# Attention softmax: mask, minimum and sign in one VectorE instruction, masks made by GpSimd

## The chip, the cores and the metric

The kernel runs on one core of one Trainium2 chip. The metric is the device time of one launch in microseconds (us), given as the median of several runs. A profiled execution is one launch recorded by the hardware profiler; its *span* reaches from its first to its last instruction, and its own time is a little longer. Five engines work side by side: TensorE (PE; its weight loads are PEld), VectorE (DVE), ScalarE (ACT), GpSimd (POOL, called Pool below) and SyncE (SP), which here only issues DMAs.

## What is computed

Two small models run in one launch, in float32, on 256 tokens of width 1024, batch 1. The first has two layers of feed-forward networks, a mixer with neighbourhood attention and an mLSTM, and a gating mixer. The second has a mixer of two attentions, a mixture of 16 experts, a mixer of two other attentions, and a second mixture. What matters here is the softmax of the five attentions, each with 8 heads of 64:

```python
# neighbourhood attention (NA): own keys in a window with a bias, and 256 context keys without one
s_loc = einsum('bqhd,baqkhd->bhqak', q_i, k_win) * scale + bias
s_ctx = einsum('bqhd,bchd->bhqc', q_i, kx) * scale
p = softmax(concatenate([s_loc, s_ctx]))
# sliding window with sinks (sw)
logits = logits - slopes * dist;  logits = where(valid, logits, -inf)
p = softmax(concatenate([logits, sink]))[..., :-1]
# causal with forget gates (fo); without them for the latent attention (la)
logits = logits + c_i[..., :, None] - cum[:, :, None, :]
p = softmax(where(pos[None, :] <= t[:, None], logits, -inf))
# selected keys (ds): the 64 best of each query by an index score
logits = logits - slopes * dist;  logits = where(dist >= 0, logits, -inf)
p = softmax(logits)
```

The slopes of `sw` and `ds` are 2 to the power -(h + 1) for head h.

## The kernel before

Each engine has a program written out by hand (`tensor_program`, `scalar_program`, `vector_program`, `pool_program`, `sync_program`), and the order in it is the order of the text. Engines wait for each other by counted semaphores: `w.wait_ge(result, ...)` waits for TensorE, `dve_out` for VectorE, `act_out` for ScalarE, `pool_out` for Pool, `const_in` and `bias_in` for DMAs. `then_inc(...)` announces an instruction's end. `behind()` on VectorE waits for all of its own earlier instructions.

The weights stream through the kernel. SyncE loads a piece into one of four `raw` buffers (512 or 2048 elements in each of 128 partitions), ScalarE copies it to `wh`, rounded to a shorter float type (L1410), VectorE takes the difference as `wl` (L2076), and TensorE multiplies with both: activations are split into `hh` and `hl` likewise, so each product is three matrix multiplications (L412). A `raw` buffer is free when `wl` is made.

An attention is a row of *units*: one head times one block of 128 queries. `NA` has 16 units with 512 keys (256 own, 256 context). `EV` has 32, 16 of `sw` and then 16 of `fo`; `OD` has 32, 16 of `la` and then 16 of `ds`. In these, the first block of queries has 128 keys and the second 256. The generator `attention(...)` stands in three programs, and `attend(n)` runs it on by n units between the pieces of the projections that go on at the same time; in `OD`, `pump(n)` puts instructions of the top-64 selection (eight largest, L2851, and their replacement, L2855) between them. For unit u:

- TensorE writes the logits into `banks[u % 2]` when the exponential of unit u-2 is done.
- VectorE adds the mask in place, in the bank: NA at L2419 with a bias that a separate instruction has summed (L2412, bias and window mask, a unit ahead), `sw` at L2766, `fo` at L2770, `la` at L2956, `ds` at L2960. Then it takes the maximum over the bank (`tensor_reduce`, L2343) and changes its sign (L2349; with sinks L2347, which takes the larger of maximum and sink too). The results lie in `st`, rows 0 and 1.
- ScalarE computes exp(bank + st row 1) into `E`, and its accumulator's sum into row 2 (L1553, which shows as two instructions).
- In step u+2 TensorE turns `E` (L649) and ScalarE copies it to `ET` (L1545); in step u+4 TensorE multiplies with the values.
- After 8 units VectorE makes reciprocals (L2360, with sinks L2356 and L2358 around an exponential of ScalarE) and scales the bank into `Y` (L2364). TensorE turns `Y` (L674), and `hl` of it is made by VectorE (L2795, L2974) for the output projection. In NA, VectorE copies the keys `kT` from a bank for each group of units (L2405); in EV ScalarE makes `e_va` and `e_vb` (L1797, L1805).

Pool loads constants (`load`, L3207), clears buffers (`zero`, L3216), keeps a ring of modulation weights filled, issues the 16 bias DMAs of NA (L3245, one in each unit, when the sum of the unit two before is done), and copies `o_kr` to `o_kz` (L3277). `phase(...)` makes it wait for the end of a phase before it loads into the room that the phase used.

Of the kernel before, what the change touches and what calls it, by code (L numbers as in the profile page):

```python
# [55 lines left out]
class Counting:  # L56
# [7 lines left out]
    tensor_tensor_scan = reciprocal = match_replace = max = nothing  # L64
# [55 lines left out]
def program(nc, dram):  # L120
# [5 lines left out]
    def sb(where, name, shape, dt=F32):  # L126
        return where.enter_context(nc.sbuf_tensor(name, shape, dt))
# [79 lines left out]
    with ExitStack() as mx:  # L207
# [4 lines left out]
        with ExitStack() as ph:  # L212
# [3 lines left out]
            na.bias = sb(ph, "bias", [P, 2, 2, T])  # L216
# [54 lines left out]
    with ExitStack() as mx:  # L271
# [16 lines left out]
        ev.on8 = sb(mx, "e_on8", [8, T])  # L288
        ev.cc = sb(mx, "e_cc", [P, 2, 8])
# [1106 lines left out]
    def scalar_program(e):  # L1396
# [139 lines left out]
        def attention(name, units, a):  # L1536
            for u in range(len(units) + 4):
# [8 lines left out]
                if u < len(units):  # L1546
# [6 lines left out]
                    e.activation(a.E[:, u % 4, 0:n], banks[u % 2][:, 0:n], ACT.Exp, bias=a.st[:, 1, c:c + 1],  # L1553
# [509 lines left out]
    def vector_program(e):  # L2063
# [34 lines left out]
        def behind():  # L2098
            w.wait_ge(dve_out)
# [232 lines left out]
        def attention(name, units, a, logits, out):  # L2332
            for u in range(len(units) + 4):
                if u < len(units):
# [4 lines left out]
                    mx, nm = a.st[:, 0, c:c + 1], a.st[:, 1, c:c + 1]  # L2339
                    w.wait_ge(result, "logit", name, u)  # L2340
                    logits(u, kd, qb, h, b)
                    behind()
                    e.tensor_reduce(mx, b[:, 0:n], AX.X, ALU.max).then_inc(*dve_out("mx", name, u))  # L2343
                    behind()
                    if kd == "sw":
                        w.wait_ge(const_in["sinks"], 0)
# [46 lines left out]
        def mixer0():  # L2393
# [21 lines left out]
            def logits(u, kd, qb, h, b):  # L2415
                if u == 0:
                    bias_sum(0)
                w.wait_ge(dve_out, "bias sum", u)
                e.tensor_tensor(b[:, 0:T], b[:, 0:T], na.bias[:, 1, u % 2, :], ALU.add).then_inc(*dve_out("biased", u))  # L2419
                if u < 15:  # L2420
                    bias_sum(u + 1)
# [6 lines left out]
            st.units = attention("na", NA, na.a, logits, out)  # L2428
# [298 lines left out]
        def even_mixer():  # L2727
# [33 lines left out]
            def logits(u, kd, qb, h, b):  # L2761
                n = P * (qb + 1)
                if kd == "sw":
                    slope = -float(np.float32(2.0) ** np.float32(-(h + 1)))
                    w.wait_ge(const_in["swdist"], 0)
                    e.scalar_tensor_tensor(b[:, 0:n], ev.swm[:, qb, 0:n], slope, b[:, 0:n], ALU.mult, ALU.add).then_inc(*dve_out("ev biased", u))  # L2766
                else:
                    w.wait_ge(const_in["causal"], 0)
                    w.wait_ge(dve_out, "ecc")
                    e.scalar_tensor_tensor(b[:, 0:n], b[:, 0:n], ev.cc[:, qb, h:h + 1], ev.cam[:, qb, 0:n], ALU.add,  # L2770
                                           ALU.add).then_inc(*dve_out("ev biased", u))
# [15 lines left out]
            st.units = attention("ev", EV, ev.a, logits, out)  # L2787
# [100 lines left out]
        def odd_mixer():  # L2888
# [63 lines left out]
            def logits(u, kd, qb, h, b):  # L2952
                n = P * (qb + 1)
                if kd == "la":
                    w.wait_ge(const_in["causal2"], 0)
                    e.tensor_tensor(b[:, 0:n], b[:, 0:n], od.cam[:, qb, 0:n], ALU.add).then_inc(*dve_out("od biased", u))  # L2956
                    return
                slope = -float(np.float32(2.0) ** np.float32(-(h + 1)))
                w.wait_ge(dve_out, "dd")
                e.scalar_tensor_tensor(b[:, 0:n], od.dd[:, qb, 0:n], slope, b[:, 0:n], ALU.mult, ALU.add).then_inc(*dve_out("od biased", u))  # L2960

            st.units = attention("od", OD, od.a, logits, lambda g: heads_of(od.Y, g % 2, 512 if g < 2 else 0))
# [239 lines left out]
    def pool_program(e):  # L3202
# [18 lines left out]

        def mod(n):
# [41 lines left out]
        pool_out.mark("ev zero")  # L3264
        for l, before in ((0, "even phase"), (1, "odd phase")):
# [247 lines left out]
```

## Time and profile before

| | us |
|---|---|
| median of 3 runs | 2475.62 (2473.22 to 2476.98) |
| profiled execution, its own time | 2474.83 |
| its span | 2472.9 |
| TensorE busy | 2328.4 (94% of the span) |
| VectorE busy | 1740.1 (70%) |
| ScalarE busy | 1197.9 (48%) |
| Pool busy | 115.7 (5%) |
| mean granted TensorE clock | 0.973 of full speed |

All times inside the execution count from the start of the span. Pool's share is that of its whole work, DMA issues among it. A `busy` of TensorE counts matrix products that wait for nothing, at whatever clock; the granted clock is 1.00 at 2.4 GHz and 0.5 at 1.2 GHz. The NA units lie between 526 and 587 us, the EV units between 1506 and 1606, the OD units between 2031 and 2090, so all the attentions together are some 220 us of the span.

In an entry such as `[1.32 <-DVE kT L2405]` the first number is the idle time in front of the instruction, and behind the arrow stands what released it.

### The profile page before, as it was taken

The numbers are of one execution on the slowest core, as the hardware profiler recorded it, in microseconds if no ns is written. First come the engines' busy times: TensorE is split into PE (matmuls) and PEld (weight loads), VectorE is DVE, ScalarE is ACT, GpSimd is POOL, SyncE is SP. The second block draws the span as 40 slices with busy tenths as digits, with TensorE's granted clock in tenths as the row PEclk, the third lists the DMA queues.
The fourth block names the chain that finished last, engine by engine and source line by source line (L and its number), as shares of the span: only waits on it lengthen the run. The fifth ranks groups of instructions, "written<-read, shape, count | busy, mean of one in ns | idle before, by whom it ended". The sixth has DMA issues, their size and how long they took to land.

```text
span 2472.9 us, 33815 instructions
## 1 busy us (share of the span) xinstructions
PE 2328.4 (94%) x14128; PEld 2038.2 (82%) x14128; DVE 1740.1 (70%) x2355; ACT 1197.9 (48%) x1549; POOL 115.7 (5%) x205
## 2 busy tenths in 40 slices
PE   7999999899989999999999998979999888899997
PEld 3778888778779999998999997868888687688886
DVE  4997777754776666666666655668888777688886
ACT  3222222334544454455554443457666555576665
POOL 0111111010000000000000010000000100000000
PEclk9999999999999999999999998989999989999999
DMA  7777887433115454455445552239988621389884
GB/s 273 230 243 254 269 265 262 130 132 110 69 58 182 171 205 169 172 205 216 153 160 177 180 199 102 99 108 330 349 311 316 259 103 52 124 341 345 317 311 167
DMA packets 80533, 501.71 MB, mean 203 GB/s; under 512 B 9584, under 2 KB 10688, under 8 KB 28656
## 3 DMA queue, kind: packets, MB, share of 16 engines
q1 hardware_dynamic: 59120, 423.66, 46.7%
q0 software_dynamic: 21248, 75.75, 9.7%
q8 instruction: 115, 1.88, 0.3%
q14 instruction: 50, 0.41, 0.1%
HBM read 498.33 MB, written 1.05 MB: 202 GB/s over the span
## 4 chain that ended last, share of the span: by engine, by line
PE 61%; DVE 22%; ACT 11%; issue 4%; DMA 2%; DVEq 0%; SPq 0%; ACTq 0%
PE bank L412 60%; DVE wl L2076 9%; ACT wh L1410 7%; DVE macc L2112 1%; ACT s L1511 1%; DVE f L2293 1%; DMA mring<-in_wmod 1%; DVE s L2284 1%; DMA raw<-in_wmod 1%; PE bank L1282 1%; DMA raw<-in_wstream 1%; DVE rs L2136 1%; PE bank L649 0%; DVE hl L2268 0%; DVE st_od L2343 0%
## 5 line engine op out<-in xcount | busy, mean ns | idle before, releaser
L2076 DVE TENSOR_TENSOR wl<-raw,wh 128x2048 fp32r<-128x2048 f32 (+1 forms) x437 | 905.0, 2077 | 378.1 <-ACT wh L1410 374.1
L1410 ACT ACTIVATE wh<-raw 128x2048 fp32r<-128x2048 f32 (+1 forms) x437 | 756.3, 1738 | 301.3 <-PE bank L412 295.1
L412 PE MATMUL bank<-hh,wh 128*128 128x258 f32 (+2 forms) x2200 | 691.7, 314 | 34.2 <-ACT o_rl L1839 5.3
L412 PE MATMUL bank<-hh,wl 128*128 128x258 f32 (+2 forms) x2200 | 675.2, 307 | 0.0
L412 PE MATMUL bank<-hl,wh 128*128 128x258 f32 (+2 forms) x2200 | 673.9, 306 | 0.0
L412 PEld LDWEIGHTS bank<-hh,wh 128*128 128x128 f32 x2200 | 422.1, 192 | 63.8 <-DVE hl L2714 6.0
L412 PEld LDWEIGHTS bank<-hl,wh 128*128 128x128 f32 x2200 | 422.6, 192 | 18.2 <-issue 0.5
L412 PEld LDWEIGHTS bank<-hh,wl 128*128 128x128 f32 x2200 | 421.1, 191 | 18.8
L412 PE MATMUL bank<-wh,hh 128*128 128x512 f32 (+1 forms) x704 | 279.2, 397 | 7.6 <-DVE wl L2076 4.7
L412 PE MATMUL bank<-wl,hh 128*128 128x512 f32 (+1 forms) x704 | 276.2, 392 | 0.0
L412 PE MATMUL bank<-wh,hl 128*128 128x512 f32 (+1 forms) x704 | 276.2, 392 | 0.0
L412 PE MATMUL bank<-H,wh 128*128 128x256 f32 (+1 forms) x704 | 218.8, 311 | 2.3 <-DVE L L2303 2.0
L412 PE MATMUL bank<-H,wl 128*128 128x256 f32 (+1 forms) x704 | 217.5, 309 | 0.0
L412 PE MATMUL bank<-L,wh 128*128 128x256 f32 (+1 forms) x704 | 217.5, 309 | 0.0
L2112 DVE SCALAR_TENSOR_TENSOR macc<-mring,c_cvec,macc 128x1024 f32<-128x1024 f32 x140 | 175.7, 1282 | 46.3 <-DMA mring<-in_wmod 41.1
L412 PEld LDWEIGHTS bank<-wh,hh 128*128 128x128 f32 x704 | 134.8, 191 | 40.2 <-issue 5.6
L412 PEld LDWEIGHTS bank<-wl,hh 128*128 128x128 f32 x704 | 134.6, 191 | 29.6
L412 PEld LDWEIGHTS bank<-wh,hl 128*128 128x128 f32 x704 | 134.7, 191 | 27.8 <-issue 0.2
L412 PEld LDWEIGHTS bank<-H,wh 128*128 128x128 f32 x704 | 132.4, 188 | 12.3 <-DVE L L2303 3.1
L412 PEld LDWEIGHTS bank<-H,wl 128*128 128x128 f32 x704 | 132.4, 188 | 8.0
L412 PEld LDWEIGHTS bank<-L,wh 128*128 128x128 f32 x704 | 132.4, 188 | 7.8
L1520 ACT ACTIVATE H<-f 128x256 fp32r<-128x256 f32 (+1 forms) x88 | 41.5, 471 | 193.0 <-DVE f L2300 151.6
(471 smaller groups left out, 2644.8 us busy)
## 6 DMA issues: line engine op xcount, KB each, us to landing
raw<-in_wstream SPq DMA_DIRECT2D x393, 1024.0 KB, 4.8
mring<-in_wmod POOLq DMA_DIRECT2D x128, 512.0 KB, 4.6
raw<-in_wmod SPq DMA_DIRECT2D x6, 1024.0 KB, 7.4
X<-in_xT SPq DMA_DIRECT2D x1, 2048.0 KB, 13.4
mods<-in_wmod SPq DMA_DIRECT2D x2, 1024.0 KB, 20.0
bias<-in_nabias POOLq DMA_DIRECT2D x16, 128.0 KB, 2.5
c_sglg<-in_sglg POOLq DMA_DIRECT2D x1, 1024.0 KB, 5.0
c_sglb<-in_sglb POOLq DMA_DIRECT2D x1, 1024.0 KB, 7.5
```

The source lines that it names most:

```text
L412: return e.matmul(out, lhsT, rhs, start=start, stop=stop, skip_group_check=True)
L1282: ins = e.transpose(banks[b][:, P * c:P * c + P], q.H[:, s_, P * c:P * c + P], ident[:])
L1410: e.activation(wh[i % NB][:, o], raw[i % NR][:, o], ACT.Copy).then_inc(*slab_high(st.split + m))
L1511: e.activation(s_, s_, ACT.Silu, bias=f.s[:, i % 2, T:T + 1]).then_inc(*act_out("silu", u, i))
L1520: e.activation(f.H[:, i - f0, :], f.f[:, i % 2, 0:n], ACT.Copy).then_inc(*act_out("H", u, i))
L2076: e.tensor_tensor(wl[i % NB][:, o], raw[i % NR][:, o], wh[i % NB][:, o].bitcast(F32), ALU.subtract).then_inc(*slab_low(st.split + m))
L2112: e.scalar_tensor_tensor(acc, src, c, acc, ALU.mult, ALU.add).then_inc(*dve_out("block", n, who))
L2136: e.reciprocal(rs[:, o:o + T], rs[:, o:o + T]).then_inc(*dve_out("rs", nm, i))
L2284: e.tensor_tensor(f.s[:, i % 2, :], banks[bank_of["fin", u, i, 0]][:, 0:W1], rs[:, 0:W1], ALU.mult).then_inc(*dve_out("rooted a", u, i))
L2293: e.scalar_tensor_tensor(f.f[:, i % 2, 0:T], f.f[:, i % 2, 0:T], f.f[:, i % 2, T:T + 1], f.s[:, i % 2, 0:T], ALU.add, ALU.mult).then_inc(* ...
```

## The change

One instruction, `tensor_tensor_reduce(bank, bank, added, -1.0, least, add, min, nm)`, stands in VectorE's program for the mask's add, the maximum and the change of sign. It writes -(logit + mask) to the bank, and the minimum of that and of the initial value `least` to row 1 of `st`. ScalarE's exponential reads the bank with a scale of -1. For `sw` the initial value is the negated sink (`e_nsk`, one small VectorE instruction for all of them), otherwise a large number.

The second operand comes ready. In NA, Pool sums bias and window mask into `added`, whose context half it clears once; it waits for the bias DMA and for `nm` of the unit two before, and issues the bias DMA of unit u+2 after the sum of unit u (the first two at the start). In EV, Pool makes the mask of each unit (`swm` times the slope; `cam` plus a column of `cc`). In OD, Pool makes those of the 16 `ds` units (`dd` times the slope) after its copy of `o_kr`; the `la` units read `cam` itself. There are two buffers, so Pool waits for `nm` of the unit two before. TensorE's program is unchanged. In the instruction counts, VectorE loses 4 for each of the 16 NA units and 3 for each of the 64 others and gains 80 and one; Pool gains 64 and one clearing.

```diff
@@ scalar_program, attention
-                    e.activation(a.E[:, u % 4, 0:n], banks[u % 2][:, 0:n], ACT.Exp, bias=a.st[:, 1, c:c + 1],
+                    e.activation(a.E[:, u % 4, 0:n], banks[u % 2][:, 0:n], ACT.Exp, bias=a.st[:, 1, c:c + 1], scale=-1.0,
@@ vector_program, attention
-                    mx, nm = a.st[:, 0, c:c + 1], a.st[:, 1, c:c + 1]
+                    added, least = mask(u, kd, qb, h, n)
                     w.wait_ge(result, "logit", name, u)
-                    logits(u, kd, qb, h, b)
-                    behind()
-                    e.tensor_reduce(mx, b[:, 0:n], AX.X, ALU.max).then_inc(*dve_out("mx", name, u))
-                    behind()
-                    if kd == "sw":
...
-                        e.tensor_scalar(nm, mx, ev.snk[:, h:h + 1], -1.0, ALU.max, ALU.mult).then_inc(*dve_out("nm", name, u))
-                    else:
-                        e.tensor_scalar(nm, mx, -1.0, None, ALU.mult).then_inc(*dve_out("nm", name, u))
+                    e.tensor_tensor_reduce(b[:, 0:n], b[:, 0:n], added, -1.0, least, ALU.add, ALU.min,
+                                           a.st[:, 1, c:c + 1]).then_inc(*dve_out("nm", name, u))
@@ vector_program, NA
-            def bias_sum(u):
...
-                e.tensor_tensor(na.bias[:, 1, u % 2, :], na.bias[:, 0, u % 2, :], na.mask[:, NA[u][1], :],
-                                ALU.add).then_inc(*dve_out("bias sum", u))
...
-                e.tensor_tensor(b[:, 0:T], b[:, 0:T], na.bias[:, 1, u % 2, :], ALU.add).then_inc(*dve_out("biased", u))
...
+            def mask(u, kd, qb, h, n):
+                w.wait_ge(pool_out, "bias sum", u)
+                return na.added[:, u % 2, :], BIG
@@ vector_program, EV
+            def mask(u, kd, qb, h, n):
+                w.wait_ge(pool_out, "mask", "ev", u)
+                w.wait_ge(dve_out, "sinks")
+                return ev.a.mask[:, u % 2, 0:n], ev.nsk[:, h:h + 1] if kd == "sw" else BIG
...
+            e.tensor_scalar(ev.nsk[:], ev.snk[:], -1.0, None, ALU.mult).then_inc(*dve_out("sinks"))
@@ vector_program, OD
+            def mask(u, kd, qb, h, n):
                 if kd == "la":
                     w.wait_ge(const_in["causal2"], 0)
...
+                    return od.cam[:, qb, 0:n], BIG
+                w.wait_ge(pool_out, "mask", "od", u)
+                return od.a.mask[:, u % 2, 0:n], BIG
@@ pool_program
+        def slot(name, u):
+            w.wait_ge(pool_out)
+            if u >= 2:
+                w.wait_ge(dve_out, "nm", name, u - 2)
+
+        def sloped(name, a, u, dist):
+            _, qb, h = (EV if name == "ev" else OD)[u]
+            n = P * (qb + 1)
+            slot(name, u)
+            e.tensor_scalar(a.mask[:, u % 2, 0:n], dist[:, qb, 0:n], -float(np.float32(2.0) ** np.float32(-(h + 1))), None,
+                            ALU.mult).then_inc(*pool_out("mask", name, u))
...
+        zero(na.added[:, :, T:2 * T], "ctx bias")
...
         for u in range(16):
+            w.wait_ge(bias_in[u % 2], u)
             if u >= 2:
...
+                w.wait_ge(dve_out, "nm", "na", u - 2)
+            w.wait_ge(pool_out)
+            e.tensor_tensor(na.added[:, u % 2, 0:T], na.bias[:, u % 2, :], na.mask[:, NA[u][1], :],
+                            ALU.add).then_inc(*pool_out("bias sum", u))
+            if u < 14:
+                bias(u + 2)
...
+        w.wait_ge(const_in["swdist"], 0)
+        for u in range(16):
+            sloped("ev", ev.a, u, ev.swm)
...
+        w.wait_ge(dve_out, "ecc")
+        for u in range(16, 32):
+            _, qb, h = EV[u]
+            n = P * (qb + 1)
+            slot("ev", u)
+            e.tensor_scalar(ev.a.mask[:, u % 2, 0:n], ev.cam[:, qb, 0:n], ev.cc[:, qb, h:h + 1], None,
+                            ALU.add).then_inc(*pool_out("mask", "ev", u))
...
                 e.tensor_copy(od.kz[64:96], od.kr[64:96, :].unsqueeze(1).to_broadcast([32, 8, T])).then_inc(*pool_out("kr placed"))
+                w.wait_ge(dve_out, "dd")
+                for u in range(16, 32):
+                    sloped("od", od.a, u, od.dd)
             phase(before)
```

## Rows read from the trace of the kernel before

**Rows 1.** the page, the chain of work that ended last, shares of the span by line.

```profile
PE bank L412 60%; DVE wl L2076 9%; ACT wh L1410 7%; DVE macc L2112 1%; ACT s L1511 1%; DVE f L2293 1%; DMA mring<-in_wmod 1%; DVE s L2284 1%; DMA raw<-in_wmod 1%; PE bank L1282 1%; DMA raw<-in_wstream 1%; DVE rs L2136 1%; PE bank L649 0%; DVE hl L2268 0%; DVE st_od L2343 0%
```

**Rows 2.** windows EV, OD-A, OD-B: busy us of each engine, clock, DMA share, GB/s.

```profile
1506.00:1606.00 100.00, 88.09 (x637) 82.75 (x636) 59.10 (x133) 43.98 (x113) 0.00 (x0) 0.95 0.25 86
2031.40:2062.90 31.50, 26.24 (x144) 23.23 (x143) 26.99 (x84) 13.90 (x51) 0.00 (x0) 0.78 0.13 46
2062.90:2090.00 27.10, 21.09 (x165) 19.36 (x165) 17.08 (x53) 15.04 (x52) 0.00 (x0) 1.00 0.12 40
```

**Rows 3.** timeline of one unit, NA and OD; start, us, operation, idle before.

```profile
557.15 0.43 DVE L2419 TENSOR_TENSOR bank<-bank,bias 128x256 f32<-128x256 f32 x1 [1.91 <-PE bank L412]
...
558.85 0.69 ACT L1553 ACTIVATE E_na<-bank,st_na 128x512 f32<-128x512 f32 x1 [0.67 <-DVE st_na L2349]
...
2048.13 0.42 DVE L2956 TENSOR_TENSOR bank<-bank,c_causal 128x256 f32<-128x256 f32 x1
...
2049.05 0.15 DVE L2349 TENSOR_SCALAR st_od<-st_od 128x1 f32<-128x1 f32 x1
...
2049.23 0.47 ACT L1553 ACTIVATE E_od<-bank,st_od 128x256 f32<-128x256 f32 x1 [1.34 <-DVE st_od L2349]
```

**Rows 4.** groups by form, VectorE and ScalarE, 500 to 2095: busy, mean ns, idle before.

```profile
L2770 DVE SCALAR_TENSOR_TENSOR bank<-bank,e_cc,c_causal 128x256 f32<-128x256 f32 x8 | 3.9, 487 | 4.0 <-PE bank L412 4.0
...
L2770 DVE SCALAR_TENSOR_TENSOR bank<-bank,e_cc,c_causal 128x128 f32<-128x128 f32 x8 | 2.8, 354 | 1.8 <-PE bank L412 1.7
...
L1553 ACT ACTIVATION_READ_ACCUMULATOR E_od<-bank,st_od 128x1 f32 x30 | 5.8, 193 | 0.0
```

**Rows 5.** timeline of TensorE at the second group of keys of NA.

```profile
567.63 0.67 PE L412 MATMUL bank<-kT,qz 128*128 128x512 f32 x1 [1.32 <-DVE kT L2405]
```

**Rows 6.** the page, DMA issues: queue, count, KB, us from issue to landing.

```profile
bias<-in_nabias POOLq DMA_DIRECT2D x16, 128.0 KB, 2.5
```

**Rows 7.** TensorE's waits in EV, 1506 to 1603: us in total, times, longest.

```profile
PE bank L412 <- ACT E_ev L1553: 2.9, 2, 2.0
PE bank L412 <- DVE hl L2795: 1.9, 1, 1.9
PE bank L412 <- DVE Y L2364: 1.5, 1, 1.5
PE bank L674 <- DVE Y L2364: 1.3, 1, 1.3
PE bank L649 <- DVE hl L2795: 1.2, 1, 1.2
```

**Rows 8.** windows inside OD-A, columns as in rows 2; the clock falls in two.

```profile
2036.50:2045.50 9.00, 5.75 (x41) 4.80 (x40) 8.26 (x31) 4.47 (x18) 0.00 (x0) 1.00 0.00 0
2045.50:2048.60 3.10, 3.10 (x13) 2.73 (x13) 2.87 (x10) 1.07 (x5) 0.00 (x0) 0.51 0.37 63
...
2055.50:2062.60 7.10, 6.54 (x27) 5.97 (x27) 5.64 (x14) 2.40 (x9) 0.00 (x0) 0.52 0.00 0
```

**Rows 9.** TensorE's waits in OD-A, 2031.4 to 2063.

```profile
PE bank L412 <- ACT E_od L1553: 4.2, 6, 1.1
```

**Rows 10.** TensorE's waits in OD-B, 2063 to 2090.5.

```profile
PE bank L412 <- ACT E_od L1553: 2.0, 3, 0.8
PE bank L412 <- DVE Y L2364: 1.6, 1, 1.6
PE bank L412 <- DVE hl L2974: 1.5, 1, 1.5
PE bank L674 <- DVE Y L2364: 0.8, 1, 0.8
```

**Rows 11.** timeline, Pool's copy and two pairs of splits on VectorE.

```profile
2012.86 1.89 POOL L3277 COPY o_kz<-o_kr 32x2048 f32<-32x2048 f32 x1 [38.04 <-DVE o_kr L2933]
...
2014.14 1.75 DVE L2076 TENSOR_TENSOR wl<-raw,wh 128x512 fp32r<-128x512 f32 x2
...
2079.24 1.29 DVE L2076 TENSOR_TENSOR wl<-raw,wh 128x512 fp32r<-128x512 f32 x2 [1.04 <-ACT wh L1410]
```

More of the change, by code:

```diff
@@ L63 @@
     tensor_tensor = tensor_scalar = scalar_tensor_tensor = tensor_copy = tensor_reduce = nothing
-    tensor_tensor_scan = reciprocal = match_replace = max = nothing
+    tensor_tensor_scan = tensor_tensor_reduce = reciprocal = match_replace = max = nothing
     def value_load(self, *a, **k):
@@ L201, in attention_room @@
         a.st = sb(where, f"st_{name}", [P, 4, units])
+        if name != "na":
+            a.mask = sb(where, f"mask_{name}", [P, 2, T])
         return a
@@ L215, in program @@
             na.vt = sb(ph, "vt", [P, 4, 512])
-            na.bias = sb(ph, "bias", [P, 2, 2, T])
+            na.bias = sb(ph, "bias", [P, 2, T])
+            na.added = sb(ph, "added", [P, 2, 2 * T])
             na.mask = const(ph, "namask", [P, 2, T])
@@ L288, in program @@
         ev.on8 = sb(mx, "e_on8", [8, T])
+        ev.nsk = sb(mx, "e_nsk", [P, 8])
         ev.cc = sb(mx, "e_cc", [P, 2, 8])
@@ L2330, in ffn, with attention @@
             run_square(next_norm.get(u, 1), n, KC - 2)
-        def attention(name, units, a, logits, out):
+        def attention(name, units, a, mask, out):
             for u in range(len(units) + 4):
@@ L2427, in mixer0 @@
             keys(0)
-            st.units = attention("na", NA, na.a, logits, out)
+            st.units = attention("na", NA, na.a, mask, out)
             for m in range(1, 4):
@@ L2786, in even_mixer @@
             e.tensor_copy(ev.rt[:], banks[bank_of["root t",]][:, 0:T:P]).then_inc(*dve_out("root t"))
-            st.units = attention("ev", EV, ev.a, logits, out)
+            w.wait_ge(const_in["sinks"], 0)
+            e.tensor_scalar(ev.nsk[:], ev.snk[:], -1.0, None, ALU.mult).then_inc(*dve_out("sinks"))
+            st.units = attention("ev", EV, ev.a, mask, out)
             for k in range(KC):
@@ L2950, in odd_mixer @@
             taken(4)
-            def logits(u, kd, qb, h, b):
-                n = P * (qb + 1)
+            def mask(u, kd, qb, h, n):
                 if kd == "la":
                     w.wait_ge(const_in["causal2"], 0)
[L2956 to L2962, printed above, removed]
+                    return od.cam[:, qb, 0:n], BIG
+                w.wait_ge(pool_out, "mask", "od", u)
+                return od.a.mask[:, u % 2, 0:n], BIG
+            st.units = attention("od", OD, od.a, mask, lambda g: heads_of(od.Y, g % 2, 512 if g < 2 else 0))
             for n in 3 * (2, 3):
```

34 lines of the change are left out of this document (9 added, 25 removed).

## The prediction

> **What bounds the kernel now.** The chain of waits comes first: 60% of it is TensorE's matrix products, and VectorE's and ScalarE's splitting of the next weights (`wl` and `wh`) is 9% and 7%; the attention's own instructions do not reach its first places [rows 1]. So a shorter softmax is worth only what TensorE waits for it. Next, the busy time of the stretches in which the attention runs [rows 2]. In the sliding and forget units (called EV, 100 us) TensorE is busy 88.1 of 100. In the first half of the last attention (OD-A, 31.5 us, the 16 `la` units, with the top-64 selection running on VectorE between them) VectorE is busy 27.0 and TensorE 26.2 of 31.5, the latter at a mean clock of 0.78. In the second half (OD-B, 27.1 us, the 16 `ds` units) they are 17.1 and 21.1. VectorE has almost no slack in OD-A, some in OD-B, much in EV. Last, TensorE's waits, one by one, below.
>
> **What one unit costs on the path.** The exponential of a unit can't start before VectorE's chain on its bank is through. Neighbourhood unit (called NA, 512 keys): 557.15 to 558.85 is 1.70 us [rows 3]. A unit of 256 keys: 2048.13 to 2049.23 is 1.10 [rows 3]. With 128 keys each of the two long instructions is 0.13 shorter, by the two widths of the forget mask (487 and 354 ns) [rows 4]: 1.10 - 0.26 = 0.84.
>
> **The new instruction.** No row shows the fused add-and-minimum. From below it is bounded by the plain add over as many elements, 0.42 at 256 [rows 3]; from above by that and ScalarE's readout of its accumulator, 0.193 [rows 4], so 0.61. The nearest row is the forget mask, which has two tensors and a pointer in one pass: 487 ns at 256, 354 at 128 [rows 4]. I take 0.49 and 0.35, and at 512 by the same step of 0.13 for each 128, 0.49 + 0.26 = 0.75. Then 0.04 until ScalarE starts, the step from the end of the last instruction to the start of the exponential in [rows 3] (2049.05 + 0.15 to 2049.23). Savings: NA 1.70 - 0.79 = 0.91; 256 keys 1.10 - 0.53 = 0.57; 128 keys 0.84 - 0.39 = 0.45. The exponential reads the bank as before; scale -1 costs it nothing. Bounds: each saving is up to 0.07 larger or 0.12 to 0.15 smaller.
>
> **NA: 0.7 us.** VectorE had itself waited 1.91 us for TensorE in front of a unit's add [rows 3], so the 16 x 0.91 = 14.6 us of freed VectorE time lies beside other work, but for one place: 1.32 us that TensorE waits for the copy of keys, queued on VectorE behind a unit and Y [rows 5]. It comes earlier by one unit's saving, less what ScalarE's exponential holds: 0.7. What becomes late instead: the mask, now Pool's. Its chain for one buffer is the sum (Pool copied 2048 elements of each partition in 1.89 [rows 11], so a 256-wide instruction is 0.24 and a fixed part, 0.35 in all, and with two inputs up to 0.6) and 2.5 from the DMA's issue to its landing [rows 6]: some 3.1 us for two units, where one unit alone took 1.91 + 1.70 = 3.6 [rows 3]. It is never late; the 16 DMAs are the same as before, issued by the same queue. The one-time clearing of the context half lies in Pool's idle time at the start. VectorE also loses its wait for these DMAs.
>
> **EV: 3.4 us.** TensorE's waits [rows 7] leave out the one for `e_vb`, ScalarE's own copy behind its split, which stays. Two waits on the exponential (2.9 together), one with 128 and one with 256 keys, shrink by 0.45 and 0.57. Two on Y (1.5, 1.3) stand behind two units in a row on VectorE, of which the first saving has partly gone into the wait before; 0.6 each. Two on `hl` (1.9, 1.2) stand behind a split that began when ScalarE's `wh` was through, and that behind an exponential: 0.6 each. 1.02 + 1.2 + 1.2 = 3.4. Ends: 1.0 if only the exponentials' waits move, 5.0 if pairs give twice.
>
> **OD-A: 6.5 us.** Eight units of each width take 8 x 0.57 + 8 x 0.45 = 8.2 us off a VectorE queue that is nearly full, with the selection's instructions behind them; 31.5 - 8.2 = 23.3 is the floor by VectorE. TensorE's floor is its busy 26.2 [rows 2], in which 3.1 + 7.1 = 10.2 us ran at 0.51 and 0.52, that is at 1.2 GHz instead of 2.4 [rows 8], with TensorE busy 9.6 of them: half of that, 4.8, comes back if the clock doesn't fall, so 21.4. The clock fell after 9.0 us in which TensorE was busy only 5.75 [rows 8]; with the 4.2 us of waits for the exponential [rows 9] cut by half it is busier there. I take one of the two stretches as gone and arrive at 25.0: 6.5 us. Ends: 4.5 (the clock falls as before: TensorE's 26.2 and some waits) and 8.2.
>
> **OD-B: 3.0 us.** Six waits (three on the exponential, 2.0; Y 1.6; `hl` 1.5; Y at the transpose 0.8) [rows 10], each behind one unit's chain: 6 x 0.5, the mean of 0.57 and 0.45. Ends 1.5 and 4.5.
>
> **Pool's new work: -1 us.** 64 mask instructions. The first masks of EV and OD are ready long ahead, later ones need only the buffer of two units ago. What Pool is moved past: the loads of the two phases after EV and OD come behind the masks in its program, but they wait for the phases' ends anyway; their price is nothing. The price lies in the SBUF: beside Pool's copy (2012.86, 1.89 us, so 0.6 us of overlap) two splits took 1.75 us, elsewhere 1.29 [rows 11], 0.46 for 0.6 of overlap. A mask of 0.35 then costs a split 0.26; if a third of 48 masks (EV and `ds`) meet one, that is 4.2 us of VectorE time, of which about the share that VectorE has where TensorE waits, a quarter, shows: 1. Ends 0 and 4.
>
> The Trainium skill has a rule here that speaks against the change (SBUF — State Buffer, § Who interferes with whom): a VectorE instruction with two SBUF inputs contends with a GpSimd instruction that reads SBUF. The trace agrees by the 1.75 against 1.29 just named. By it the new fused instruction, with one input in PSUM, would be free of it, and only the splits would pay, which is the sum above.
>
> **The sum.** 0.7 + 3.4 + 6.5 + 3.0 - 1.0 = 12.6 us off the profiled execution's 2474.83, 2462.2. That execution is 0.8 under the median of the runs, 2475.62, so 2463.0 for the median.
>
> **Rivals.** (a) The fused instruction takes a second, separate one to write its minimum, as ScalarE's exponential does: 0.193 more in each unit [rows 4]. Savings 0.72, 0.38 and 0.26: NA 0.5, EV 2.3, OD-A 31.5 - 27.5 = 4.0, OD-B 6 x 0.3 = 1.8, less 1.0: 7.6, so 2468.0. For it: that row; against: plain VectorE reductions write their result in the same instruction [rows 3]. 0.15. The Trainium skill says as much (VectorE: DVE Perf Modes, § Two Vector instructions with no wait between them): an op that also writes its accumulator is two instructions, the main one and a read. No row of the trace before shows it for VectorE.
>
> (b) The waits stay because the splits set them. `wh` and then `wl` of one tile follow each other, 16% of the chain [rows 1]; a shorter unit only lets VectorE wait longer for `wh`. Then EV keeps 1.0 of its 3.4, OD-B 0.5, NA nothing, and OD-A, whose pace the selection sets, 3.0: 4.5, so 2471.1. For it: the `hl` and Y waits stand right behind splits. Against: VectorE busy 27.0 of 31.5 in OD-A [rows 2]. 0.16.
>
> (c) Slower: Pool's reading and VectorE's splits block each other in EV and OD-B, wholly and on the path. Price: the 0.46 of [rows 11] for each of 48 masks, 22 us; 2475.6 - 13.6 + 22.1 = 2484.1. It decides the sign from 13.6 / 48 = 0.28 us a mask, and is slower than the bound from 0.39. For: that the two splits were slowed nearly one for one. Against: the masks are a fifth as long as that copy, and in OD-B the splits are few. 0.09.
>
> **Chances and range.** Forecast 0.60 (its own range 2457 to 2468), (a) 0.15, (b) 0.16, (c) 0.09. 0.2% of the median, 5 us, is about what a measurement tells from no change; its bound is 2470.7. Faster by more: 0.58 + 0.13 + 0.06 = 0.77; within: 0.15; slower: 0.08. Bottom of the range: all upper ends together would be 2475.6 - (0.9 + 5.0 + 8.2 + 4.5) = 2457, and 2 more for the second clock stretch: 2455. Top: (a) and (b) are inside up to 2472; (c) and the tails are left out.
>
> **What would show it.** The fused instruction as one row of about 490, 350 and 750 ns, exponentials starting about 0.53 us after it begins, at 256 keys. OD-A near 25 us, with VectorE at about 19 us busy and one clock stretch at 0.5 gone. EV at 96 to 97 with the `hl` and Y waits shorter; `e_vb` unchanged. Pool masks of 0.3 to 0.5 us. A second row beside each fused one would show (a); unchanged Y and `hl` waits (b); splits of over 2.5 us beside masks, or waits on `mask` or `added` in the rows of VectorE (c). The prediction is wrong if a mask takes Pool over 1.7 us, a `ds` unit's time in OD-B (27.1 / 16), or if OD-A keeps over 28 us.

## The result

The changed kernel takes 2451.26 us, median of 4 runs (2445.76 to 2452.92), against 2474.42 of the kernel before in the same session; ratio 0.9898, 95% interval 0.9887 to 0.991. That is 23 us faster; 12.6 were forecast, and the time lies below the range (2455 to 2472). Its profiled execution took 2445.76 us, span 2444.0, the fastest of its runs, so that the profiles differ by 29.1 us and the medians by 23.2.

Of the engines (share of the span, before in brackets) TensorE is at 95% (94), VectorE at 69% (70), ScalarE at 49% (48), Pool at 7% (5); the granted clock is 0.978 (0.973). The chain that ended last, in answer to [rows 1]:

```profile
PE bank L416 63%; DVE wl L2080 8%; ACT wh L1414 6%; DVE macc L2116 1%; ACT s L1515 1%; DVE f L2297 1%; DMA mring<-in_wmod 1%; DVE s L2288 1%; PE bank L653 1%; DMA raw<-in_wmod 1%; DVE rs L2140 1%; PE bank L1286 1%; DVE hl L2272 0%; ACT H L1524 0%; DVE tmpm L2265 0%
```

TensorE's share has grown from 60% to 63%, and the splits (the two instructions that make `wh` and `wl` of the next weights) have gone from 7 and 9 to 6 and 8. The fused instruction stands, by form, as follows (busy, mean ns; idle before), in answer to [rows 4]:

```profile
L2345 DVE CUSTOM_DVE_ANT_0 bank<-bank,added 128x512 f32<-128x512 f32 x16 | 11.1, 698 | 27.3 <-PE bank L416 27.3
...
L2345 DVE DVE_READ_ACCUMULATOR2_ANT st_od<- 128x1 f32 x32 | 4.5, 141 | 0.0
...
L2345 DVE CUSTOM_DVE_ANT_0 bank<-bank,mask_ev,e_nsk 128x256 f32<-128x256 f32 x8 | 3.7, 489 | 0.1
L2345 DVE CUSTOM_DVE_ANT_0 bank<-bank,mask_od 128x256 f32<-128x256 f32 x8 | 3.5, 432 | 1.3 <-PE bank L416 1.2
...
L2345 DVE CUSTOM_DVE_ANT_0 bank<-bank,mask_od 128x128 f32<-128x128 f32 x8 | 2.4, 300 | 4.0 <-PE bank L653 3.0 <-PE bank L416 1.0
```

```profile
L3246 POOL TENSOR_TENSOR added<-bias,c_namask 128x256 f32<-128x256 f32 x16 | 13.7, 855 | 50.4 <-DVE st_na L2345 40.7 <-issue 5.0 <-DMA bias<-in_nabias 2.7
L3278 POOL TENSOR_SCALAR mask_ev<-c_causal,e_cc 128x256 f32<-128x256 f32 x8 | 9.3, 1157 | 12.5 <-DVE st_ev L2345 10.9 <-DVE st_ev L2357 1.5
...
L3208 POOL TENSOR_SCALAR mask_od<-o_dd 128x256 f32<-128x256 f32 x8 | 6.8, 850 | 6.9 <-DVE st_od L2345 5.5 <-DVE st_od L2357 1.2
...
L3208 POOL TENSOR_SCALAR mask_od<-o_dd 128x128 f32<-128x128 f32 x8 | 4.3, 533 | 47.5 <-DVE st_od L2345 46.7 <-DVE st_od L2357 0.7
```

It is two rows each time: the main one (432 ns at 256 keys, 489 where the initial value is a pointer, 300 at 128, 698 at 512) and a readout of 0.14. Pool's masks take far more than the 0.35 forecast: 0.53 to 0.93 where nothing holds them. The means of 1.16 and 0.86 come of one mask and one sum of over 2.7 us, which are looked at below. EV's first mask, made long before its use beside other instructions of VectorE, took 1.94. In the windows NA, ahead of EV, EV, OD-A and OD-B (same work as in [rows 2], bounded by the same instructions of TensorE):

```profile
527.86:587.29 59.43, 58.62 (x330) 45.30 (x329) 20.79 (x43) 24.28 (x51) 16.81 (x26) 1.00 0.25 80
1491.52:1503.34 11.82, 9.67 (x78) 9.07 (x77) 6.90 (x9) 3.82 (x4) 0.00 (x0) 1.00 0.69 258
1503.34:1592.05 88.71, 82.95 (x637) 78.45 (x636) 43.74 (x101) 43.81 (x113) 24.09 (x30) 1.00 0.28 98
2015.15:2037.70 22.55, 21.25 (x144) 18.89 (x143) 20.26 (x69) 13.77 (x50) 0.00 (x0) 0.93 0.15 61
2037.70:2060.43 22.73, 20.69 (x165) 19.32 (x164) 11.22 (x40) 14.88 (x52) 9.37 (x14) 1.00 0.14 48
```

The time that TensorE doesn't work is the length less its busy time: in EV 88.71 - 82.95 = 5.8 us, where [rows 2] had 11.9; in OD-A 1.3 (5.3), in OD-B 2.0 (6.0), in NA 0.8 (2.1, by the window below). The clock stands at 1.00 in EV (0.95) and at 0.93 in OD-A (0.78). TensorE's waits in EV and OD-A, in answer to [rows 7] and [rows 9]:

```profile
PE bank L416 <- ACT e_vb L1809: 2.2, 1, 2.2
PE bank L416 <- ACT E_ev L1557: 1.2, 1, 1.2
PE bank L416 <- DVE hl L2775: 0.8, 1, 0.8
PE bank L416 <- DVE Y L2361: 0.8, 1, 0.8
PE bank L653 <- DVE hl L2775: 0.6, 1, 0.6
```

```profile
PE bank L416 <- ACT E_od L1557: 0.7, 2, 0.5
PE bank L416 <- DVE Y L2361: 0.4, 1, 0.4
```

The kernel before, in two windows not shown earlier, NA and the 16 us ahead of EV:

```profile
526.17:587.08 60.91, 58.85 (x331) 45.19 (x330) 34.71 (x75) 25.34 (x51) 7.51 (x14) 1.00 0.24 82
1490.07:1506.05 15.98, 13.81 (x78) 12.79 (x77) 6.83 (x8) 3.82 (x4) 0.00 (x0) 0.69 0.54 194
```

### The profile page after: what moved, and what is told of

It is laid out like the page before. It is cut to its first block, busy times and chain, and to the rows that moved or that the text cites. A ratio compares the mean times of both kernels' runs of the same rounds, so it can differ in the third digit from the quotient of the medians.

```text
span 2444.0 us, 33909 instructions
## 1 busy us (share of the span) xinstructions
PE 2316.0 (95%) x14128; PEld 2026.8 (83%) x14128; DVE 1696.2 (69%) x2260; ACT 1197.4 (49%) x1549; POOL 168.0 (7%) x270
## 4 chain that ended last, share of the span: by engine, by line
PE 65%; DVE 19%; ACT 10%; issue 4%; DMA 1%; DVEq 0%; SPq 0%; ACTq 0%
PE bank L416 63%; DVE wl L2080 8%; ACT wh L1414 6%; DVE macc L2116 1%; ACT s L1515 1%; DVE f L2297 1%; DMA mring<-in_wmod 1%; DVE s L2288 1%; PE bank L653 1%; DMA raw<-in_wmod 1%; DVE rs L2140 1%; PE bank L1286 1%; DVE hl L2272 0%; ACT H L1524 0%; DVE tmpm L2265 0%
```

## The experiments

All ratios are to the kernel before in the same session. In the stretch table below, idle is a window's length less TensorE's busy time, and low is the time at 1.2 GHz instead of 2.4, by the clock's record in each profile (twice the length times what the granted clock lacks to 1.00, within rounding).

**The parts one by one.** A switch in the changed kernel gives each attention either the fused instruction and Pool's masks or the three instructions of the kernel before.

```diff
-                    e.tensor_tensor_reduce(b[:, 0:n], b[:, 0:n], added, -1.0, least, ALU.add, ALU.min, ...
+                    if name == "ev":      # "od", "na", or "ev" and "od"
+                        e.tensor_tensor_reduce(b[:, 0:n], b[:, 0:n], added, -1.0, least, ALU.add, ALU.min, ...
+                    else:
+                        logits(...); behind(); e.tensor_reduce(...); behind(); e.tensor_scalar(...)   # as before
```

> The change in the EV units alone (sliding and forget attention); NA and OD keep VectorE's three instructions on the bank and Pool makes no mask for them. Theory A (VectorE's shorter row of instructions ends TensorE's waits; in the trace of the changed kernel they fell by 6.2 us in EV, and the two low-clock stretches inside EV, worth 3.1 us, went with them): 9 us faster than before, ratio 0.9963. Rival (the EV term of the forecast was right and the rest of the gain there is a clock that falls at other times by chance): 3.4 us, ratio 0.9986. A rival by which the whole clock gain from 1490 us on belongs to EV: 15 us, ratio 0.994.

Measured: 2467.23 against 2475.66, ratio 0.9968 (0.9958 to 0.9978): 8 us faster. The interval is 5.4 to 10.4 us: theory A's 9 lies in it, the forecast's 3.4 and the third theory's 15 lie outside.

> The change in the OD units alone (latent and selected attention). Theory A: TensorE's waits fell by 8.0 us there in the changed kernel, and the clock returned some 3 more: 10 us faster than before, ratio 0.996 (9 to 13). Rival (half of it is the clock's chance): 6 to 8 us, ratio 0.997. If the parts add, only_ev, only_od and 1.5 us for NA make up the 23 us between the medians.

Measured: 2465.45, ratio 0.9958 (0.9947 to 0.997): 10 us faster (7.4 to 13.1). This too is theory A's, though 8 us, the upper end of its rival, is not excluded. It is also what the forecast had for the two halves of OD together, 9.5.

> The change in the neighbourhood units alone. Theory A: TensorE's idle time in NA falls from 2.1 to 0.8 us and nothing else moves: 1.3 us faster, within what can be told from nothing, ratio 0.9995 (0.998 to 1.001). The rival that NA's 15 us of freed VectorE time pay more than its waits: 4 us or more, ratio under 0.9985; it would close the gap between the two parts measured, 8.4 and 10.2 us, and the whole, 25.

Measured: 2475.52 against 2475.68, ratio 0.9999 (0.9989 to 1.0008): nothing that can be told (2.7 us faster to 2.0 slower). TensorE's idle time in NA fell as expected (59.42 us long, 0.8 idle).

> The change in EV and OD together, NA as before. If the parts add (8.4 and 10.2 us measured alone): 18.6 us faster, ratio 0.9925. If the whole (23 to 25 us) holds something that comes only of EV and OD together: 23 us, ratio 0.991. If it is NA that brings the rest in company (its low-clock stretch of 10 us ahead of EV was missing wherever NA was changed): 18 us and again 10 us of low clock between 1490 and 1506 us.

Measured: 2452.22 against 2477.2, ratio 0.9896 (0.988 to 0.9913): 25 us, all of the gain without NA. The parts alone gave 18.6, with intervals that reach from 13 to 23.5 in sum; the whole's reaches from 21.5 to 29.7. So they may just add, and the medians don't settle it. By the stretches they do add: EV's and OD's windows are as long here (90.8, 22.6, 22.7) as in the kernels with one part changed.

**Offloading or the row.**

> Pool makes all masks as in the changed kernel, but VectorE keeps three instructions in a row on the bank: a plain add of the ready mask, the maximum, and the change of sign. Theory A (the shorter row in front of the exponential is what pays): no gain, within 2 us of before, or up to 4 us slower by Pool's reading beside the splits; ratio 0.9995 to 1.002. Rival B (what pays is work moved off VectorE to Pool): at least a third of the 23 us, ratio 0.997 or less.

```diff
-                    e.tensor_tensor_reduce(b[:, 0:n], b[:, 0:n], added, -1.0, least, ALU.add, ALU.min, ...
+                    e.tensor_tensor(b[:, 0:n], b[:, 0:n], added, ALU.add) ...
+                    behind()
+                    e.tensor_reduce(mx, b[:, 0:n], AX.X, ALU.max) ...
+                    behind()
+                    e.tensor_scalar(nm, mx, -1.0, None, ALU.mult) ...
```

Measured: 2472.39 against 2475.66, ratio 0.999 (0.9978 to 1.0002): at most 5.4 us faster, and possibly nothing. The third of the gain that rival B needs, 7.7 us, is excluded. TensorE's idle times stay: 11.4 us in EV, 7.6 and 6.4 in OD.

> The fused instruction as in the changed kernel, but VectorE makes the masks itself, a unit ahead, behind each unit's fused instruction; Pool does no mask at all. Theory A: VectorE has 44 of 89 us idle in EV, so nearly all of the gain stays, only the masks of the second unit of a pair delay what is queued behind them: 17 to 21 us faster than before, ratio 0.992. Rival B (offloading pays): half of the gain is lost, 10 to 12 us, ratio 0.9955. A rival by which Pool's reading cost the changed kernel some us on the splits: 23 us or more.

```diff
 # VectorE, behind the fused instruction of unit u (NA and OD's ds units alike); Pool makes no mask
+                w.wait_ge(dve_out, "nm", "ev", u - 1)
+                e.tensor_scalar(ev.a.mask[:, (u + 1) % 2, 0:n], ev.swm[:, qb, 0:n], slope, None, ALU.mult) ...
```

Measured: 2450.49 against 2475.66, ratio 0.9898 (0.9885 to 0.9911): 25 us, as much as the changed kernel. The 0.22 to 0.35 us of each mask on VectorE cost TensorE 0.4 us of idle time in EV (6.2 against 5.8) and 0.5 in OD-B. Rival B is out: what pays is not what moved to Pool. I had expected a loss of 2 to 6 us, which the interval doesn't show. By its number the result is the third rival's (23 us or more, because Pool's reading costs the changed kernel something on the splits), but the splits speak against it: the nine `wl` of EV take 2.29 us each on average in the kernel before, in the changed one and here.

**The length of the row, in doses.**

> The changed kernel with one small instruction put back into the row of each unit: the fused one writes its minimum to row 0, and a second one of 0.15 us, behind a wait for it, copies it to row 1, from where ScalarE takes it. The exponential of a 256-key unit should start 0.7 us after the fused instruction (0.51 in the changed kernel, 1.10 before). Theory A (the gain follows the length of that row): a third of the gain goes, 15 us faster than before, ratio 0.994. Rival (it is the number of VectorE's instructions or the masks' place that counts, not the row): 22 us or more stay, ratio 0.991 or less.

```diff
-                                           a.st[:, 1, c:c + 1]).then_inc(*dve_out("nm", name, u))
+                                           mx).then_inc(*dve_out("mx", name, u))
+                    behind()
+                    e.tensor_scalar(nm, mx, 1.0, None, ALU.mult).then_inc(*dve_out("nm", name, u))
```

Measured: 2458.22 against 2475.68, ratio 0.9934 (0.9919 to 0.9948): 17.5 us faster (13 to 20), where theory A had 15 and the rival 22 or more; in the same session the changed kernel 22.8. A 256-key unit's exponential starts 0.70 us after the fused instruction, as expected. A 128-key unit in OD-A, from the fused instruction to the exponential:

```profile
2019.78 0.29 DVE L2354 CUSTOM_DVE_ANT_0 bank<-bank,c_causal 128x128 f32<-128x128 f32 x1
2019.99 0.14 DVE L2354 DVE_READ_ACCUMULATOR2_ANT st_od<- 128x1 f32 x1
2020.17 0.15 DVE L2357 TENSOR_SCALAR st_od<-st_od 128x1 f32<-128x1 f32 x1
...
2021.22 0.29 DVE L2354 CUSTOM_DVE_ANT_0 bank<-bank,c_causal 128x128 f32<-128x128 f32 x1
```

```profile
2020.36 0.37 ACT L1559 ACTIVATE E_od<-bank,st_od 128x128 f32<-128x128 f32 x1 [1.05 <-DVE st_od L2357]
```

The same in the kernel before and in the changed one:

```profile
2036.39 0.29 DVE L2956 TENSOR_TENSOR bank<-bank,c_causal 128x128 f32<-128x128 f32 x1
...
2038.10 0.29 DVE L2956 TENSOR_TENSOR bank<-bank,c_causal 128x128 f32<-128x128 f32 x1
```

```profile
2037.23 0.37 ACT L1553 ACTIVATE E_od<-bank,st_od 128x128 f32<-128x128 f32 x1 [1.32 <-DVE st_od L2349]
```

```profile
2019.14 0.29 DVE L2345 CUSTOM_DVE_ANT_0 bank<-bank,c_causal 128x128 f32<-128x128 f32 x1
...
2020.39 0.29 DVE L2345 CUSTOM_DVE_ANT_0 bank<-bank,c_causal 128x128 f32<-128x128 f32 x1
```

```profile
2019.53 0.37 ACT L1557 ACTIVATE E_od<-bank,st_od 128x128 f32<-128x128 f32 x1 [0.61 <-DVE st_od L2345]
```

2019.78 to 2020.36 is 0.58 us, where the kernel before has 0.84 (2036.39 to 2037.23) and the changed one 0.39 (2019.14 to 2019.53). From unit to unit it is 1.44 us (2019.78 to 2021.22), against 1.71 (2036.39 to 2038.10) and 1.25 (2019.14 to 2020.39). Each 0.19 or 0.26 in the row is 0.19 or 0.27 in the pace. TensorE's idle times follow in the same order (table below): OD-A 7.6, 3.7, 1.3; EV 11.9, 7.6, 5.8.

**The profiles once more.**

> The changed kernel once more, in five rounds and with a second profile. In its first profile no low clock was granted between 1491 and 1592 us, where the profile before had 10.1 us ahead of EV's first unit and 10.4 us in EV. Theory A: TensorE's idle times repeat to a tenth (0.8 in NA, 5.8 in EV, 1.3 in OD-A, 2.0 in OD-B), and the low stretches ahead of EV and in it come and go by chance; 20 to 24 us faster, ratio 0.991. Rival (the clock stays up because of the change): no low stretch again from 1490 to 1592 us, and 25 us or more.

Measured: 2452.89 against 2475.68, ratio 0.9907 (0.9891 to 0.9924); idle times of 0.8, 5.8, 1.4 and 2.0 us again. One low stretch of 3.4 us fell in EV, none ahead of it. So the idle times repeat as theory A had it, but not its second half, by which the low stretches would come and go by chance: with 0 and 3.4 us in EV both profiles of the changed kernel lie far under the 10.4 and 10.7 of the kernel before.

> The kernel before once more, for a second profile. Theory A: TensorE's idle time is again 2.1 in NA, 11.9 in EV and 6 in OD-B; in OD-A it is 7.6 if only one short low-clock stretch falls there (31.4 us long with three, 29.8 with one, as the two experiments with three instructions had). Rival (three low stretches in OD-A belong to the kernel before): 14 us of low clock again.

Measured: 2476.81 in one run. OD-A is 29.78 us long and 7.6 idle, with 2.8 us of low clock:

```profile
2033.06:2062.84 29.78, 22.22 (x144) 18.95 (x143) 26.54 (x83) 13.66 (x50) 0.00 (x0) 0.95 0.13 47
2062.84:2090.32 27.48, 21.15 (x164) 19.41 (x164) 17.42 (x54) 15.14 (x52) 0.00 (x0) 1.00 0.10 39
```

Profiles by stretch: length, idle, low, in us.

| kernel | ahead of EV | EV | OD-A | OD-B |
|---|---|---|---|---|
| before | 16.0, 2.2, 10.1 | 100.0, 11.9, 10.4 | 31.4, 5.3, 14.1 | 27.1, 6.0, 0 |
| before, second | 15.9, 2.2, 9.8 | 100.1, 11.9, 10.7 | 29.8, 7.6, 2.8 | 27.5, 6.3, 0 |
| NA alone | 11.8, 2.2, 0 | 99.2, 11.3, 10.2 | 29.8, 7.6, 2.6 | 27.5, 6.4, 0 |
| OD alone | 15.9, 2.2, 9.8 | 100.1, 11.9, 10.7 | 22.6, 1.4, 3.0 | 22.7, 2.0, 0 |
| three instructions, Pool's masks | 13.5, 1.1, 6.7 | 101.3, 11.4, 15.5 | 29.8, 7.6, 2.6 | 27.6, 6.4, 0 |
| EV alone | 12.8, 2.2, 2.2 | 90.8, 5.8, 4.6 | 29.8, 7.6, 2.7 | 27.5, 6.3, 0 |
| EV and OD | 12.7, 2.2, 2.0 | 90.8, 5.8, 4.8 | 22.6, 1.4, 3.0 | 22.7, 2.0, 0 |
| masks by VectorE | 13.5, 1.1, 6.7 | 91.5, 6.2, 5.2 | 22.6, 1.5, 2.7 | 23.2, 2.5, 0 |
| one step put back | 11.8, 2.2, 0 | 90.7, 7.6, 0 | 25.2, 3.7, 2.8 | 24.5, 3.5, 0 |
| changed | 11.8, 2.2, 0 | 88.7, 5.8, 0 | 22.5, 1.3, 3.1 | 22.7, 2.0, 0 |
| changed, second | 11.8, 2.2, 0 | 90.1, 5.8, 3.4 | 22.6, 1.4, 3.0 | 22.7, 2.0, 0 |
| each mask twice (below) | 11.8, 2.1, 0 | 90.1, 5.9, 3.4 | 22.6, 1.4, 2.9 | 24.0, 3.1, 0 |
| each mask four times (below) | 13.5, 1.1, 6.7 | 122.6, 27.4, 25.8 | 22.5, 1.2, 3.8 | 37.7, 12.8, 8.6 |

**How much Pool may take.**

> The changed kernel with each mask of EV and OD made twice over by Pool (two equal instructions in a row, the second behind a wait for the first); NA is left as it is. A mask is then 1.1 us (128 keys) or 1.7 us (256) of Pool, against 1.42 us for a unit in OD-B and 2.8 in EV. Theory A (Pool works beside the path until its time for a mask passes a unit's): EV as in the changed kernel, OD-B 1 to 3 us longer by its 256-key units; 20 to 23 us faster than before, ratio 0.9915. Rival (masks made ahead already cost the changed kernel time, by contention or lateness): each further mask costs as much again, 5 us or more lost, ratio 0.993 or more.

```diff
             slot(name, u)
+            e.tensor_scalar(a.mask[:, u % 2, 0:n], ...).then_inc(*pool_out("first mask", name, u))
+            w.wait_ge(pool_out)
             e.tensor_scalar(a.mask[:, u % 2, 0:n], ...
```

Measured: 2450.46 against 2477.2, ratio 0.9887 (0.9869 to 0.9905). It is 23.5 to 32.5 us faster than before, so nothing is lost. OD-B is 23.95 us long against 22.73, within the 1 to 3 us expected, and VectorE waits 5.4 us in all for masks.

> The same with four equal instructions for each mask of EV and OD: 2.1 and 3.4 us of Pool. Theory A: 8 x 2.1 + 8 x 3.4 = 44 us of Pool in OD-B against its 22.7, so OD-B some 17 us longer (two masks are made ahead of it); in EV 93 us against 89, some 8 us longer; 2475 to 2482, no faster than before, ratio 1.000 (0.998 to 1.003). Rival (TensorE's projections hide late masks): ratio under 0.996.

Measured: 2510.26, ratio 1.0127 (1.0109 to 1.0145): 33 us slower than before, where 2475 to 2482 was expected. VectorE now waits for masks:

```profile
DVE bank L2359 <- POOL mask_ev L3387: 33.6, 13, 3.6
DVE bank L2359 <- POOL mask_od L3307: 20.8, 10, 3.3
DVE bank L2359 <- POOL mask_ev L3307: 15.1, 8, 3.1
```

OD-B is 37.7 us long, 15.0 more than in the changed kernel (17 expected); EV is 122.6, 33.9 more (8 expected). In EV I had compared Pool's 93 us in all with the stretch's 89, but each mask is due at its own unit, two units come close together, and Pool can be no more than two masks ahead. So the total isn't the bound; the wait at each pair is. The forecast had named 1.7 us of Pool for a mask as the point from which it would be wrong: at 1.1 and 1.7 us (128 and 256 keys) nothing is lost, at 2.1 and 3.4 more than the whole gain.

## Why the prediction was wrong

**The unit's row: right.** The forecast had 0.53 us from the fused instruction to the exponential at 256 keys; it is 0.51 (2028.14 to 2028.65):

```profile
2028.14 0.42 DVE L2345 CUSTOM_DVE_ANT_0 bank<-bank,c_causal 128x256 f32<-128x256 f32 x1
2028.65 0.47 ACT L1557 ACTIVATE E_od<-bank,st_od 128x256 f32<-128x256 f32 x1 [0.76 <-DVE st_od L2345]
```

At 128 it had 0.39, and it is 0.39. Rival (a) was right on the form and wrong on the price: there is a second row of 0.14, but the main one is shorter than taken (432 against 490), and the next instruction of VectorE doesn't wait for the readout:

```profile
1531.02 0.48 DVE L2345 CUSTOM_DVE_ANT_0 bank<-bank,mask_ev,e_nsk 128x256 f32<-128x256 f32 x1
1531.42 0.14 DVE L2345 DVE_READ_ACCUMULATOR2_ANT st_ev<- 128x1 f32 x1
1531.42 0.49 DVE L2345 CUSTOM_DVE_ANT_0 bank<-bank,mask_ev,e_nsk 128x256 f32<-128x256 f32 x1
```

The second unit's instruction starts at 1531.42 with the readout of the first; from unit to unit it is 0.40 us. With the row of three it had been 1.04 (1539.39 to 1540.43 in the kernel before). The Trainium skill (VectorE: DVE Perf Modes, § Two Vector instructions with no wait between them) has the two instructions, and these rows agree.

**EV: 3.4 forecast, 6.1 of waits and some 4 of clock.** This is the step that failed. Each wait was to shrink by about one unit's saving (0.45 to 0.6), `e_vb` not at all, and the clock stood at nothing. The seven waits shrank by 0.6 to 1.3 us, by 0.9 on average. Here is the loop in front of the first one, 2.00 us before, 1.22 after:

```profile
1509.98 0.30 DVE L2766 SCALAR_TENSOR_TENSOR bank<-c_swdist,bank 128x128 f32<-128x128 f32 x1 [1.96 <-PE bank L412]
...
1513.18 2.29 DVE L2076 TENSOR_TENSOR wl<-raw,wh 128x2048 fp32r<-128x2048 f32 x1 [2.33 <-ACT wh L1410]
1515.39 0.29 DVE L2766 SCALAR_TENSOR_TENSOR bank<-c_swdist,bank 128x128 f32<-128x128 f32 x1
```

```profile
1510.89 0.37 ACT L1553 ACTIVATE E_ev<-bank,st_ev 128x128 f32<-128x128 f32 x1 [2.38 <-DVE st_ev L2347]
...
1511.24 1.90 ACT L1410 ACTIVATE wh<-raw 128x2048 fp32r<-128x2048 f32 x1
...
1516.29 0.37 ACT L1553 ACTIVATE E_ev<-bank,st_ev 128x128 f32<-128x128 f32 x1 [2.98 <-DVE st_ev L2347]
```

```profile
1505.73 0.36 DVE L2345 CUSTOM_DVE_ANT_0 bank<-bank,mask_ev,e_nsk 128x128 f32<-128x128 f32 x1 [1.17 <-PE bank L416]
...
1508.48 2.29 DVE L2080 TENSOR_TENSOR wl<-raw,wh 128x2048 fp32r<-128x2048 f32 x1 [2.33 <-ACT wh L1414]
1510.69 0.35 DVE L2345 CUSTOM_DVE_ANT_0 bank<-bank,mask_ev,e_nsk 128x128 f32<-128x128 f32 x1
```

```profile
1506.18 0.37 ACT L1557 ACTIVATE E_ev<-bank,st_ev 128x128 f32<-128x128 f32 x1 [1.13 <-DVE st_ev L2345]
...
1506.54 1.91 ACT L1414 ACTIVATE wh<-raw 128x2048 fp32r<-128x2048 f32 x1
...
1511.13 0.37 ACT L1557 ACTIVATE E_ev<-bank,st_ev 128x128 f32<-128x128 f32 x1 [2.53 <-DVE st_ev L2345]
```

Unit by unit, VectorE's row lets ScalarE's exponential go, behind which `wh` stands in ScalarE's program, behind that the split `wl`, and behind that the next unit's row and its exponential, for which TensorE waits. From the first unit's row to the split it was 3.20 us (1509.98 to 1513.18) and is 2.75 (1505.73 to 1508.48): 0.45. From the second's row to its exponential it was 0.90 (1515.39 to 1516.29) and is 0.44 (1510.69 to 1511.13): 0.46. Two units lie in series, and 0.78 of their 0.91 came off the wait. The wait for `e_vb` that I had left out, as ScalarE's own, has such a loop in front of it too: from the last row ahead of it that a `wh` stands behind to `e_vb` it was 6.66 us (1519.26 to 1525.92) and is 5.76 (1514.25 to 1520.01), 0.90 less, and the wait lost 0.8. In sum: the exponentials' two waits went from 2.9 to 1.2, Y's from 2.8 to 0.8, `hl`'s from 3.1 to 1.4 and `e_vb`'s from 3.0 to 2.2, which is 6.2. That two units lie in series is shown for the first wait and for `e_vb`'s; for the others it is inferred from how much they lost. The split, which rival (b) had as what keeps the waits, is what handed the savings on.

The second half of the miss is the clock in EV, which the sum didn't price. Five profiles in which EV keeps three instructions have 10.2 to 15.5 us at 1.2 GHz in it; the seven that fuse them (the doubled masks with 3.4 among them, the fourfold ones left aside) have 0 to 5.2. With TensorE busy nearly throughout, half of the difference of some 8 us is time, an estimate that two profiles of the changed kernel bear out roughly: with the same idle time, 3.4 us of low clock made EV 1.4 us longer (90.1 against 88.7). That the clock stays up where TensorE waits less is what the forecast had said of OD-A alone. Why it stays up here isn't shown: among the kernels that fuse, low clock doesn't follow the idle time (7.6 us idle and none low with one step put back, 5.8 and 4.6 with EV alone).

The span and mean granted clock of every run say the same of the whole. By them the time at low clock is 132 us on average in 45 runs of the kernel before and 120 in nine of the changed one. Among those 45 runs a microsecond more of low clock goes with 0.31 more of span, and at most it costs 0.5, so that 12 us less are worth some 4 to 6, an estimate. The idle time that went (6.1 in EV, 6.2 and 4.3 in OD against the second profile of before, 1.3 in NA) is 18, and both together make the 23 us.

**OD-A: 6.5 forecast, 7.2.** Right in size, in part by luck. The profile from which the forecast was made had 14.1 us of low clock there (10.2 in the two stretches that the forecast counted, and the end of one that began earlier), and none of the others, changed or not, has over 3.8. So its clock was no part of the gain: nothing "came back". At 1.2 GHz TensorE's work is longer and its waits shorter (5.3 against 7.6 us idle), which had made a case of 31.4 us out of the usual 29.8. What was gained is 29.8 - 22.6 = 7.2, or 0.45 for each of the 16 units. From the profile of the forecast it was 31.4 - 22.5 = 8.9, past the forecast's upper end of 8.2 and under its floor of 23.3 us by VectorE. That was no floor: VectorE was busy 27.0 of the 31.5 us and had idle time to give as well.

**OD-B: 3.0 forecast, 4.4 to 4.8.** The six waits went from 5.9 us to 2.0, 0.65 each where 0.5 was forecast. How many units stand behind each of them wasn't followed. **NA: 0.7 forecast, 1.5 by the windows** (60.91 to 59.43), and nothing by its own runs. One wait for `kT` of 0.6 us is gone that hadn't been counted.

**Pool: 1 us of cost forecast, none measured.** The masks take twice what was estimated and more, and VectorE never waits for one; doubled, they cost nothing that can be told. And the splits don't pay:

```profile
1575.54 2.77 POOL L3278 TENSOR_SCALAR mask_ev<-c_causal,e_cc 128x256 f32<-128x256 f32 x1 [1.89 <-DVE st_ev L2345]
1578.68 0.93 POOL L3278 TENSOR_SCALAR mask_ev<-c_causal,e_cc 128x256 f32<-128x256 f32 x1 [0.37 <-DVE st_ev L2345]
```

```profile
1575.23 2.29 DVE L2080 TENSOR_TENSOR wl<-raw,wh 128x2048 fp32r<-128x2048 f32 x1
```

A mask that starts at 1575.54, with a split of 1575.23 under way, takes 2.77 us where its like takes 0.93; the split takes 2.29 as everywhere. In the other order, Pool's copy first and the split second, the split pays [rows 11]. Whoever comes second waits. The Trainium skill's rule (SBUF — State Buffer, § Who interferes with whom), that such a pair contends and that issue order decides who blocks, agrees with these rows; what I had taken from it was the contention without the order. In the changed kernel such meetings are rare. The forecast had a third of the 48 masks of EV and `ds` meet a split. One did in earnest, the one above, and Pool waited. Four more still had 0.06 to 0.27 us to go when a split began (at 1565.89, 2052.07, 2055.30 and 2058.27), and these splits took 2.29 us, 1.29 for a pair, and 0.69 as usual. One of NA's sums also came second: it began at 502.64, with a split of 502.50 under way, and took 2.75 us in place of 0.72. The second profile has the same meetings. In all of them it is Pool that waits, and Pool has the time. The fused instruction, which the forecast had taken as free of contention because one of its inputs lies in PSUM, was: one at 572.00, beside a sum of Pool (571.80, 0.72 us), took the usual 0.70.

**The range** was too narrow because its lower end added the forecast's own upper ends, in which EV stood with 5.0 and no clock. With 6.1 and 4 for EV, 7.2, 4.6 and 1.5 the sum is 23, as measured between the medians. Between the second profiles (spans 2475.0 and 2447.4) it is 27.6, by another 4 from the stretch ahead of EV, which is the first open end.

**What stays open.** Ahead of EV, where no attention runs, the profiles have between 0 and 10 us of low clock: 10 in both of the kernel before and in OD alone, 2 in EV alone and in EV and OD, and where NA was changed none in five and 6.7 in three (Pool's masks with three instructions, masks by VectorE, fourfold masks). That stretch is 16.0 us long with 10 of low clock and 11.8 with none. But NA alone is no faster at its median, though its profile, the fastest of its 12 runs, is 7 us under it. So the clock there varies between runs of one kernel, and what it gives to the medians isn't known. The profiled runs of the changed kernel are the fastest and the second fastest of theirs. OD alone gained 10.2 where its stretches lost 12 (7.2 and 4.8), which its interval allows; but its six runs have 139 us of low clock on average, against 131 in the runs of the kernel before beside them, so that some of its gain may have gone to low clock elsewhere. The version with masks by VectorE is as fast as the changed kernel and leaves Pool free; none was found that beats both.

## What to carry to other kernels

Follow a wait back through every engine of its loop and count how often the shortened piece lies in it. In the two waits followed here it lay there twice, and the seven waits of EV gave 0.9 us on average where one unit saves about half a microsecond. Where the clock falls in a stretch with waits, take a second profile before its low stretches enter a sum, as a cost or as a gain. A fused instruction paid by its place in front of another engine's work, and not by the work that it took off VectorE; moving masks to Pool brought nothing that could be told.

## What the runs showed of the hardware

VectorE's readout of its accumulator, 0.14 us, runs beside the next VectorE instruction if nothing waits for it: two 256-key instructions of 0.48 us followed each other in 0.40. Pool's multiply by a constant takes 0.53 us at 128 columns and 0.85 at 256, its two-input add 0.72 at 256 where nothing holds it, and its copy of 2048 columns in 32 partitions took 1.89. A Pool instruction that started while a split ran on VectorE was held for the rest of it (2.77 against 0.93 us, 2.75 against 0.72), and a split that started during Pool's copy took longer too (1.75 against 1.29 for the pair), but splits that began in the last 0.06 to 0.27 us of a mask did not.
